# A second mixer whose projection starts with the index keys, with its late scalings split between ScalarE and GpSimd

## The reference

```python
cq, ckv, kidx, widx, dq, dk, dv = split_cols(hn @ od_w_in[j], OD_WIDTHS)
o_c = dsa_mixer(cq, ckv, kidx, widx, ...)      # picks keys by an index score, then attends
o_d = diff_attention(dq, dk, dv, ...)          # 4 heads, each the difference of two softmaxes
mix = concatenate([o_c, o_d]) @ od_w_out[j]

# dsa_mixer
cq, ckv = rms_norm(c_q, q_norm), rms_norm(c_kv, kv_norm)
q_idx = (cq @ w_qidx)                          # 4 index heads of 64
score = sum over heads of relu(q_idx . k_idx) * w_idx, masked causally by blocks of 64
idx = top_k(score, 128)                        # the 128 best keys of each query
# then softmax attention of 8 heads over the chosen keys only, in the latent space
```

## Time and profile before

| what | value |
|---|---|
| median of 3 runs | 1954.14 us |
| the profiled execution, its own time | 1956.61 us |
| its span in the trace | 1954.8 us |
| granted TensorE clock, mean over the span | 0.994 of full speed |
| TensorE busy | 98% of the span |
| VectorE, ScalarE, GpSimd busy | 53%, 33%, 15% of the span |
| projection of the second mixer, in the trace | about 1281 to 1402 us |
| groups after it and the output projection | about 1402 to 1522 us |

### The profile page before, as it was taken

The page is one execution under the profiler, slowest core; times in us unless marked ns, Lnnn a source line. Parts: engine busy times, 40 slices in busy tenths (PEclk is TensorE's granted clock), DMA queues, the critical chain, the costliest instruction groups (busy, mean ns, idle before and its releaser), DMA issues.

```text
span 1954.8 us, 24237 instructions
## 1 busy us (share of the span) xinstructions
PE 1917.9 (98%) x8980; PEld 1546.9 (79%) x8980; DVE 1028.6 (53%) x1502; ACT 636.4 (33%) x959; POOL 288.2 (15%) x221
## 2 busy tenths in 40 slices
PE   8999999999999999999999999999989999999997
PEld 6888888777888888887888888877657888888885
DVE  5444477664645442347544542369984644442345
ACT  5332222244323222224322322234573423222222
POOL 2000001311300000224000000162243200000225
PEclk9999999999999999999999999999999999999998
DMA  5323223322222323322322233331101323322321
GB/s 174 106 86 107 97 98 102 88 87 82 88 94 87 111 92 107 108 76 88 104 91 93 88 114 99 97 116 65 54 1 44 108 86 98 105 97 97 108 75 54
DMA packets 56730, 179.59 MB, mean 92 GB/s; under 512 B 12144, under 2 KB 12144, under 8 KB 56656
## 3 DMA queue, kind: packets, MB, share of 16 engines
q1 hardware_dynamic: 54656, 173.69, 27.6%
q0 software_dynamic: 928, 3.02, 0.5%
q10 hardware_dynamic: 1088, 2.10, 0.3%
HBM read 175.04 MB, written 3.15 MB: 91 GB/s over the span
## 4 chain that ended last, share of the span: by engine, by line
PE 91%; DVE 4%; POOL 2%; ACT 1%; issue 1%; DMA 0%; POOLq 0%; SPq 0%; DVEq 0%; ACTq 0%
PE ps L1799 57%; PE ps L1816 25%; PE ps L2244 2%; PE ps L1906 1%; POOL sumsq L1276 1%; POOL square L1274 1%; PE ps L2144 1%; PE ps L2162 1%; DVE sm L1004 0%; PE ps L2193 0%; DVE t L504 0%; PE ps L2177 0%; PE ps L1957 0%; PE ps L1826 0%; PE ps L2003 0%
## 5 line engine op out<-in xcount | busy, mean ns | idle before, releaser
L1799 PE MATMUL ps<-x_hi,w_hi 128*128 128x512 f32 x1728 | 683.1, 395 | 10.7 <-ACT w_hi L357 7.4
L1799 PE MATMUL ps<-x_lo,w_hi 128*128 128x512 f32 x1728 | 675.3, 391 | 0.0
L1799 PE MATMUL ps<-x_hi,w_lo 128*128 128x512 f32 x1728 | 675.3, 391 | 0.0
L365 DVE TENSOR_TENSOR w_lo<-raw,w_hi 128x1024 fp32r<-128x1024 f32 x310 | 396.9, 1296 | 409.2 <-ACT w_hi L357 403.3
L357 ACT ACTIVATE w_hi<-raw 128x1024 fp32r<-128x1024 f32 x322 | 332.3, 1050 | 341.1 <-PE ps L1816 293.6
L1799 PEld LDWEIGHTS ps<-x_hi,w_hi 128*128 128x128 f32 x1728 | 326.0, 189 | 85.0 <-ACT w_hi L357 7.4
L1799 PEld LDWEIGHTS ps<-x_lo,w_hi 128*128 128x128 f32 x1728 | 326.2, 189 | 68.8 <-issue 2.4
L1799 PEld LDWEIGHTS ps<-x_hi,w_lo 128*128 128x128 f32 x1728 | 326.0, 189 | 68.8 <-DVE w_lo L365 0.8
L1816 PE MATMUL ps<-act_hi,w_hi 128*128 (+1 forms) x720 | 280.3, 389 | 0.0
L1816 PE MATMUL ps<-act_hi,w_lo 128*128 (+1 forms) x720 | 280.1, 389 | 0.0
L1816 PE MATMUL ps<-act_lo,w_hi 128*128 (+1 forms) x720 | 280.1, 389 | 0.0
(11 more groups left out here) (360 smaller groups left out, 1322.0 us busy)
## 6 DMA issues: line engine op xcount, KB each, us to landing
raw<-in_weights SPq DMA_DIRECT2D x322, 512.0 KB, 3.4
h<-in_xT ACTq DMA_DIRECT2D x4, 512.0 KB, 6.8
out<-result SPq DMA_DIRECT2D x4, 512.0 KB, 3.0
p_raw<-in_pT POOLq DMA_DIRECT2D x2, 512.0 KB, 4.0
scratch_u<-u_sc SPq DMA_DIRECT2D x1, 512.0 KB, 6.6
u_grp<-scratch_u SPq DMA_DIRECT2D x1, 512.0 KB, 4.1
scratch_y<-y_grp SPq DMA_DIRECT2D x2, 256.0 KB, 3.1
y_ch<-scratch_y SPq DMA_DIRECT2D x1, 512.0 KB, 3.6
```

Source lines behind the costliest of these rows:

```text
L365: dve.tensor_tensor(w_lo[:, slot], raw[:, slot], w_hi[:, slot].bitcast(F32), SUB)\
L1799: last = pe.matmul(ps[:, bank], w[:, slot, k], x[:, k], start=(k == 0 and part == 0), stop=(k == KD - 1 and part == 2))
```

## The change

Three things are done together in the second mixer, and nothing else is touched.

- The projection begins with the index keys: `OD_IN_ORDER` starts (3, 0, 1, 2), so place 0 is `kidx`/`widx`, places 1 and 2 are `cq`, place 3 is `ckv`. The product for the index queries (`query_index`) moves into the middle of chunk 3, and the index scores, their relu and `combine` move one chunk earlier.
- VectorE no longer scales places 4 to 15. ScalarE copies each from PSUM to SBUF (`evict`), and GpSimd multiplies it there by `rstd`; the multiplication of the latents by their norms moves from VectorE to GpSimd as well. TensorE waits for the copy (`z_raw`) before it reuses a bank, and for the multiplication (`z_ready`) before it uses the values.
- The steps of the selection are spread anew: 49 of the 54 stand in the projection instead of 35, and the last five after groups 13, 15, 17, 19 and 21.

```diff
-OD_IN_ORDER = (0, 1, 2, 3) + tuple(4 * kind + i for i in range(4) for kind in (1, 2, 3))
+OD_IN_ORDER = (3, 0, 1, 2) + tuple(4 * kind + i for i in range(4) for kind in (1, 2, 3))
...
-SELECTS = {4: 1, 6: 1, 7: 5, 8: 5, 9: 4, 10: 4, 11: 4, 12: 3, 13: 4, 14: 4}
-GROUP_SELECTS = {12: 2, 13: 2, 14: 2, 15: 2, 16: 1, 17: 1, 18: 1, 19: 1, 20: 1, 22: 1, 23: 1, 24: 1,
-                 25: 1, 26: 1, 27: 1}
+SELECTS = {3: 1, 4: 4, 5: 1, 6: 5, 7: 6, 8: 5, 9: 5, 10: 4, 11: 5, 12: 4, 13: 4, 14: 4, 15: 1}
+GROUP_SELECTS = {13: 1, 15: 1, 17: 1, 19: 1, 21: 1}
...
             for j in range(OD_IN):
-                scale(j)
+                if j < 4:
+                    scale(j)
...
+                left = SELECTS.get(j, 0)
+                if j == 4:
+                    select(left)
+                    left = 0
                 if j == 5:
                     latent_root(1)
-                if j in (4, 5):
+                if j in (3, 4, 5):
                     dve.wait_ge(od_s["const"], 2)
-                    combine(j - 4)
+                    combine(j - 3)
                 if j == 4:
                     latent_root(0)
-                if j == 6:
-                    latents()
...
-            pool.wait_ge(z_ready, z_base(5) + 3)
+            pool.wait_ge(z_ready, z_base(5) + 4)
...
-            for j in range(DVE_AHEAD, OD_IN + 2):
-                split_lo(pool, first, AHEAD + j)
+            pool.wait_ge(rstd_ready, 6)
+            for j in range(4, OD_IN):
+                pool.wait_ge(od_s["z_raw"], j - 3)
+                hh, kind = divmod(j - 4, 3)
+                dst = (dq, dk, dv)[kind][:, hh % 2]
+                pool.tensor_tensor(dst, dst, rstd[:], MULT).then_inc(z_ready, 1)
+                split_lo(pool, first, AHEAD + DVE_AHEAD + j - 4)
+                if j == 9:
+                    pool.wait_ge(od_s["rstd"], 2)
+                    pool.wait_ge(od_s["qidx_done"], 2)
+                    for i, x in enumerate((cq[:, 0], cq[:, 1], ckv[:])):
+                        pool.tensor_tensor(x, x, (std, sumsq)[i // 2][:], MULT)\
+                            .then_inc(od_s["latent"], 1)
...
+            def evict(j):
+                hh, kind = divmod(j - 4, 3)
+                act.wait_ge(chunk_used, first + j + 1)
+                if hh >= 2 and kind < 2:
+                    act.wait_ge(od_s["scores"], 2 * NQ * (hh - 1))
+                if hh >= 2 and kind == 2:
+                    act.wait_ge(od_s["dv_turned"], hh - 1)
+                act.activation((dq, dk, dv)[kind][:, hh % 2], ps[:, od_bank(j)], ACT.Copy)\
+                   .then_inc(od_s["z_raw"], 1)
+
             for j in range(OD_IN):
+                if j >= 4:
+                    evict(j)
                 split_hi(act, first, AHEAD + 2 + j)
...
-                if j in (4, 5, 6):
-                    relus(j - 4)
+                if j in (3, 4, 5):
+                    relus(j - 3)
...
             for j in range(OD_IN):
-                if j >= 4:
-                    pe.wait_ge(z_ready, zb + (j - 3 if j < 6 else j - 1))
+                if j in (4, 5):
+                    pe.wait_ge(z_ready, zb + j - 3)
+                if j >= 6:
+                    pe.wait_ge(od_s["z_raw"], j - 5)
                 inside = {at: k for k, at in groups_of_chunk(j).items()}
                 in_chunk(pe, first, j, od_bank(j), n=5 if j == 0 else None,
-                         between=lambda at: group(inside[at]) if at in inside else None)
+                         between=lambda at: query_index() if (j, at) == (3, 4) else
+                         group(inside[at]) if at in inside else None)
...
                 if j == 3:
-                    query_index()
-                if j == 4:
                     index_weights()
-                if j in (4, 5, 6):
-                    index(j - 4)
+                if j in (3, 4, 5):
+                    index(j - 3)
```

34 lines of the change are left out of this document (9 added, 25 removed).

## The result

The changed kernel took **1964.84 us** (median of 4 runs, 1964.27 to 1967.38) against 1954.1 us of the kernel before on the same chip (1952.67 to 1954.2, 4 runs): ratio 1.0054, 95% interval 1.004 to 1.0067. It is slower by 10.7 us, over twice what a measurement can tell, and outside the range forecast (1950.8 to 1960.0).

A forecast was written before the change was run, and what follows sets the result against it. TensorE is busy 98% of the span, and VectorE's list was taken to set the pace in the tail. Lateness +5.8 at group 13 less 5.0 given back made +0.8 us on 1954.14, stated as 1955.0 us, range 1950.8 to 1960.0.

The forecast's parts named there:

- Part 1: VectorE's relief: twelve scalings of 0.69 us and three latent multiplications go, idle 4.41 and 0.87 us before index work filled.
- Part 2: Projection start: mask of group 0 at 1332.8 with six selection steps before it, including 2.0 us of blocking.
- Part 3: Projection: mask of group 12 comes 75.0 us after that of group 0; even undisturbed, TensorE 1.3 us late at group 13.
- Part 4: Projection: GpSimd's instructions block VectorE for 4.5 us, between 1 and 9, making TensorE 5.8 us late at group 13.
- Part 5: Tail, groups behind the projection: with five steps left, waits of 6.3 us shrink, giving back 5.0 us, between 3 and 7.
- Part 6: The rest at nothing or little: ScalarE's twelve copies, index queries in chunk 3 (0, at most 1.1), last head's values (0).
- B: Slower: VectorE held up at mixes and running sums of chunks 7 to 15, blocking past 7.6 us; 1960; chance 0.20.
- C: Tail is a chain of latencies, not VectorE's load: gives back 2.5 us, total 1957.4; counted within the forecast's 0.64.
- A: Port free when VectorE needs it: blocking 1 us or less, tail gives 6 to 7, 1949.5 to 1950.2 us; chance 0.16.
- D: Middle of chunk 3 waits for gained weights: +1.1 us on TensorE, nothing on VectorE, 1956; counted within the forecast's 0.64.

The follow-up runs named there:

- e1: The change with the two selection tables as in the kernel before (35 steps up to the mask of group 12, 19 after); 1956.71 us, ratio 1.0007.
- e2: The kernel before with the change's new selection tables alone, the step of chunk 3 put at chunk 4; 1975.64 us, ratio 1.0102.
- e6: The change with 13 late selection steps (second to fourteenth of the third selection) left out of the computation; 1964.85 us, ratio 1.0044.
- e10: The change with the first eight units of the second kind normalised on VectorE instead of GpSimd; ratio 1.0041.
- e13: The change with its last five selection steps, all those in the tail, left out of the computation; ratio 1.0030.
- e8: The change with 13 selection steps of 384 keys and the last five steps left out of the computation; 1959.6 us, ratio 1.0024.
- e11: The change with its five tail steps placed at groups 12, 13, 13, 14, 15, nothing left out; ratio 1.0039.
- e3: The change without GpSimd's twelve multiplications by rstd, left out of the computation; 1962.51 us, ratio 1.0040.
- e12: The change with tables of 39 steps before the mask of group 12 and the tail's steps ending at group 23; 1958.03 us, ratio 1.0013.
- e5: The change with tables of 41 steps before the mask of group 12, between the old 35 and the change's 49; 1960.1 us, ratio 1.0023.

## Why the prediction was wrong

The sum was +5.8 − 5.0; the trace shows +12.1 − 1.3. Every term had the right sign, and three were mis-sized, all in one direction.

**Part 1, right and worth nothing by itself.** The scalings and the earlier index work did free VectorE: 6 us idle in e1, 10.5 us between e2 and the change.

**Part 2, the mask of group 0 at 1332.8: 3.5 us too early.** It came at 1332.97, which is 1336.3 on the clock of before (3.33 us are added to times of the page). The rows give the pieces:

```profile
1304.55 3.19 DVE L364 TENSOR_TENSOR w_lo<-raw,w_hi 128x1024 fp32r<-128x1024 f32 x2
1307.66 1.26 DVE L930 SCALAR_TENSOR_TENSOR kept<-relu,stat,causal 128x256 f32<-128x256 f32 x1
...
1327.02 3.59 DVE L930 SCALAR_TENSOR_TENSOR kept<-relu,stat,kept 128x512 f32<-128x512 f32 x3
...
1331.50 1.38 DVE L910 SCALAR_TENSOR_TENSOR sc<-sc 128x1 f32<-128x1 f32 x1
...
1332.97 0.29 DVE L989 CUSTOM_DVE_ANT_0 sm<-ps,causal 128x128 f32<-128x128 f32 x1
```

Chunk 3 ended when I said (1303.94 on the page, 1307.3) and the first combine ended 1.0 us late. The second combine has 384 keys and took 2.7, where I gave it the 2.2 of the first. In the third GpSimd's next multiplication and low part began (1328.76 to 1332.86 on the page), and it took 4.3 instead of 3.3, and lambda's single product 1.4 instead of 0.2. I had put 2.0 us of blocking at one place of this stretch and none at the two others, though the rule I had stated applied to them.

**Part 3, right.** The masks of groups 0 and 12 are 82.2 us apart. Taking off what was blocked between them (2.15 + 0.9 + 0.95 + 0.9 + 2.1, the five instructions that were held up, 7.0 us) leaves 75.2; I had worked out 75.0. What the sum over twelve groups hid is where it falls: TensorE was 4.5 us late at its turn in group 4 and 8.7 at that in group 6, since ten of the fourteen steps are due by chunk 8. Of the 8.7, 1.5 are the half clock; e6, e10 and e13 have 7.2 there. An early lateness is not made good later when VectorE never idles, so the total came out the same.

**Part 4, 4.5 us of blocking: 7.0.** Inside my bounds of 1 to 9. The term was counted from meetings of mixes and running sums. One mix was held up, for 1 us, and neither running sum (0.69 and 0.96 us); the two longest were other closing steps:

```profile
1346.45 2.50 DVE L973 TENSOR_SCALAR kept<-kept,stat 128x256 f32<-128x256 f32 x1
...
1383.88 1.47 DVE L958 SCALAR_TENSOR_TENSOR kept<-rank,stat,kept 128x384 f32<-128x384 f32 x1
1385.39 2.63 DVE L962 TENSOR_TENSOR work<-work,kept 128x384 f32<-128x384 f32 x1
```

The first and the third lie beside low parts of GpSimd (1346.39 and 1384.90), the second beside a multiplication. Held up were two-operand instructions and a comparison of one tensor with a scalar; maximum steps, reciprocals and masks from PSUM were not.

The Trainium skill, "SBUF — State Buffer", section "Who interferes with whom", names both kinds as able to contend with GpSimd: instructions of VectorE with two SBUF inputs, and `tensor_scalar` (with copies and casts) in a two-port mode, though not the form that also writes out its accumulator. Of a two-port mode it says that whichever engine issues first gets the shared ports for its whole instruction, and the other is blocked. The trace agrees that either engine can be the one that waits: 2.50 us on VectorE instead of 0.35, and 2.09 us on GpSimd in the tail instead of 0.76.

**Part 5, the tail gives back 5.0: 1.3.** This is the largest miss, 3.7 us. For a tail without steps the term is 1.0 too high, 4.0 in e13 and 3.9 in e8, and so in e11, with all of them done by group 15. The step that failed is that I counted the five remaining steps by their load. One of them, the closing step at group 19, cost GpSimd 1.3 us and TensorE a wait of 1.41. I looked for GpSimd holding VectorE up, and never for the opposite. The last 1.4 us or so are the half clock behind the next wait, 1.19 us; e3, with the same waits, did without it, so this part of the miss is the luck of one execution. The prediction had no term for it.

**Part 6, right** for ScalarE: no wait for a copy before a chunk. The values of the last head waited 1.5 us for GpSimd (1412.17), and TensorE then stood another 0.42 us for the mix, so it was hidden, as I had it, behind a VectorE that was later still. In e1, without that cover, the same wait is 1.1 us, where it was 0.57 before, and the whole lateness is 1.3.

Together: 3.5 + 2.5 + 3.7 = 9.7 of the 10.0 us between forecast (+0.8) and trace (+10.8).

Of the signs, three failed by their numbers: the mask of group 0 at 1336.3 instead of 1332 to 1334, that of group 12 (1415.14 on the page) at 1418.5 instead of 1410 to 1414, and the waits for GpSimd at 3.5 us instead of 1 or 2. TensorE's waits for masks and mixes in the projection, 6.6 us, were as said.

**The rivals.** B had the right side and the right mechanism, VectorE held up by GpSimd, and its condition held only with the start taken in: blocking of 7.0 us from the mask of group 0 on stays under its 7.6, and the start 3.5 late passes it. Of its place, the mixes and running sums of chunks 7 to 15, one mix came true. It kept the tail's 5.0 and so gave 1960. C, the tail gives back 2.5, was nearer than my 5.0 to the 1.3 measured, for a reason of which only the floor is right: with no step in the tail 2.4 us of waits for GpSimd stay (e13), but VectorE's steps count above it. Both came true in part and together, and I had treated them as alternatives; B with C is 1962.5. A was out: TensorE did wait. D did not happen: the first gained weights took 1.84 us instead of 3.40, and nothing waited in chunk 3. At 0.20 for slower the chances were too bold, given three unknown costs that all added to one side.

## What to carry to other kernels

Before moving work into a stretch where the receiving engine is full, add it up for each deadline and not over the stretch: ten of fourteen steps were due by the ninth of sixteen chunks, and the engine could not make that good. Then look at the time left over at each deadline: here e1 shows VectorE idle for 4.3 and 1.4 us before two early masks and for 0.2 and 0.8 before two late ones. Four more steps fitted (e12), six did not where I put them (e5), and fourteen were asked for. When GpSimd and VectorE share a stretch, list every instruction of both that reads two operands from SBUF or compares a tensor with a scalar, in both directions, and put the steps that were not held up (here the maximum steps) where they meet.
